# Second layer's modulation summed on VectorE beside the gate/up product, instead of by matmuls on TensorE

## What is computed

```python
c_act = jax.nn.silu(c)[:, None, :]
cc_act = jax.nn.silu(c_ctx)[None, None, :]
for i in range(DEPTH):                       # DEPTH = 2
    need_ctx_out = i < DEPTH - 1
    mx = jnp.split(c_act @ ada_w[i] + ada_b[i], 6, axis=-1)     # ada_w[i]: 1024 x 6144
    mc = jnp.split(cc_act @ ada_w[i] + ada_b[i], 6, axis=-1)
    h_x = modulate(rms_norm(x, norm1_g[i]), mx[0], mx[1])
    h_c = modulate(rms_norm(y_ctx, norm1_g[i]), mc[0], mc[1])
    ...
    x = x + mx[2] * out_x
    x = x + mx[5] * swiglu(modulate(rms_norm(x, norm2_g[i]), mx[3], mx[4]), ffn_w_in[i], ffn_w_out[i])
```

## Time and profile before

| | |
|---|---|
| median of 3 runs | 2474.78 us (2474.26 to 2474.81) |
| the profiled execution | 2470.74 us |
| its span in the profile | 2468.8 us |
| TensorE busy | 2395.5 us (97%), 14666 matmul records |
| VectorE busy | 1507.4 us (61%) |
| ScalarE busy | 1213.8 us (49%) |
| GpSimd busy | 145.5 us (6%) |
| moved by DMA | 398.29 MB, mean 161 GB/s |

### The profile page before, as it was taken

How to read it: one execution, slowest core, us unless ns; L and a number is a source line. 1 busy time by engine, 2 the same in 40 slices (tenths; PEclk the granted TensorE clock), 3 DMA queues, 4 the chain that set the end, 5 groups by cost and what they waited for, 6 DMA issues and landing times.

```text
span 2468.8 us, 40542 instructions
## 1 busy us (share of the span) xinstructions
PE 2395.5 (97%) x14666; PEld 2063.5 (84%) x14666; DVE 1507.4 (61%) x2244; ACT 1213.8 (49%) x1776; POOL 145.5 (6%) x121
## 2 busy tenths in 40 slices
PE   7998999999899988999999999999999999999999
PEld 6745788888788857888888999898888899989887
DVE  5376533322552466766776847777677666677875
ACT  4365422222343524654654577555555545865553
POOL 3000100000000000000000012010000000221000
PEclk9999999999999999999999999999999999999999
DMA  9485632333243414656665555356566565544654
GB/s 328 152 266 183 214 110 93 93 98 94 81 128 94 146 50 137 188 183 191 179 188 190 177 171 179 112 175 185 181 192 186 184 189 165 173 134 145 198 171 149
DMA packets 397629, 398.29 MB, mean 161 GB/s; under 512 B 17344, under 2 KB 394720, under 8 KB 397520
## 3 DMA queue, kind: packets, MB, share of 16 engines
q1 hardware_dynamic: 394656, 390.25, 51.4%
q0 software_dynamic: 2864, 6.58, 0.8%
HBM read 395.73 MB, written 1.05 MB: 161 GB/s over the span
## 4 chain that ended last, share of the span: by engine, by line
PE 90%; DVE 5%; ACT 2%; issue 2%; DMA 0%; POOL 0%; SPq 0%; DVEq 0%; ACTq 0%
PE acc L1014 27%; PE acc L1025 25%; PE acc L1018 23%; PE wk L1089 2%; PE acc L1089 2%; DVE w_lo L2170 2%; PE wk L1197 1%; PE acc L1525 1%; PE acc L1232 1%; PE wk L1232 1%; PE acc L1108 1%; PE wk L1215 1%; PE acc L1434 1%; PE wk L1434 1%; PE wk L1108 1%
## 5 line engine op out<-in xcount | busy, mean ns | idle before, releaser
L2170 DVE TENSOR_TENSOR w_lo<-raw,w_hi 128x1024 fp32r<-128x1024 f32 (+1 forms) x656 | 816.7, 1258 | 563.4 <-ACT w_hi L1573 561.8
L1573 ACT CAST w_hi<-raw 128x1024 fp32r<-128x1024 f32 (+1 forms) x650 | 664.1, 1034 | 481.5 <-PE acc L1025 373.4
L1025 PE MATMUL acc<-h_all,w_lo 128*128 128x256 f32 (+1 forms) x3696 | 575.0, 298 | 0.0
L1018 PE MATMUL acc<-h_all,w_hi 128*128 128x256 f32 (+1 forms) x3360 | 556.0, 318 | 11.1 <-DVE rot L2486 4.9
L1025 PEld LDWEIGHTS acc<-h_all,w_lo 128*128 128x128 f32 x3696 | 525.0, 191 | 40.5
L1018 PEld LDWEIGHTS acc<-h_all,w_hi 128*128 128x128 f32 x3360 | 487.9, 192 | 55.4 <-issue 13.5
L1014 PE MATMUL acc<-h_all,w_hi 128*128 128x512 f32 x2016 | 509.0, 395 | 4.5 <-DVE h_all L2294 4.5
L1014 PEld LDWEIGHTS acc<-h_all,w_hi 128*128 128x128 f32 x2016 | 365.0, 190 | 70.5 <-issue 4.7
L1014 PE MATMUL acc<-hid_all,w_hi 128*128 128x512 f32 x880 | 221.5, 392 | 0.0
L1014 PEld LDWEIGHTS acc<-hid_all,w_hi 128*128 128x128 f32 x880 | 156.8, 188 | 26.8
L1025 PEld LDWEIGHTS acc<-hid_all,w_lo 128*128 128x128 f32 x1056 | 152.6, 188 | 17.1
(11 more groups left out here) (390 smaller groups left out, 2180.7 us busy)
## 6 DMA issues: line engine op xcount, KB each, us to landing
raw<-in_w_in_dram SPq DMA_DIRECT2D x100, 512.0 KB, 4.0
raw<-in_ffn_w_in_dram SPq DMA_DIRECT2D x88, 512.0 KB, 3.6
raw<-in_ffn_w_gate_dram SPq DMA_DIRECT2D x88, 512.0 KB, 4.1
raw<-in_ffn_w_up_dram SPq DMA_DIRECT2D x88, 512.0 KB, 4.2
raw<-in_ffn_w_down_dram SPq DMA_DIRECT2D x80, 512.0 KB, 4.1
ring<-in_ada_w_dram SPq DMA_DIRECT2D x58, 512.0 KB, 5.9
raw<-in_ret_w_qkvg_dram SPq DMA_DIRECT2D x48, 512.0 KB, 3.6
raw<-in_ffn_w_out_dram SPq DMA_DIRECT2D x40, 512.0 KB, 3.4
```

Of the source, the lines that this page charges most:

```text
L1018: pe.matmul(outs[cb], w_hi[:, s, k, c], x[:, kk, t], start=(u == 0 and k == 0 and x is hi), stop=False, skip_group_check=True)
L1025: mm = pe.matmul(o, w_lo[:, s, k, cb * P:(cb + 1) * P], x[:, u * KCH + k, t], start=False, stop=(last and k == nk - 1), skip_group_check=True)
L1573: act.copy(w_hi[:, s, 0:nk, :], raw[:, s, 0:nk, :]).then_inc(hi_done, 1)
L2170: dve.tensor_tensor(w_lo[:, s, 0:nk, :], raw[:, s, 0:nk, :], w_hi[:, s, 0:nk, :], ALU.subtract).then_inc(lo_done, 1)
```

## The change

The second layer's 48 units leave TensorE's side stream. Their weights are loaded by GpSimd in 48 chunks of 128 rows by 1024 columns (512 KB each) into two new buffers `ada_l`; a load waits until the chunk two before has been used. VectorE multiplies each chunk by the column of c_act that belongs to its 128 rows and adds it up over the eight chunks of a vector: 8 sums (m = 0 and 1 for both conditions, m = 2 to 5 for x alone), 64 operations of 1024 columns, placed in gu0 after step and evacuation of units 4 to 11 and 16 to 23 (one chunk, two operations each) and 28 to 43 (two chunks, one operation each). The 128 partitions of each sum are added on TensorE by four matmuls, after gu0's units 11, 23 (two sums each), 31, 35, 39 and 43, 32 in all. They are turned after dn0's unit 3 and finished by VectorE after its unit 8. The sums lie in `rows`, so the three tables ahead, behind and since are loaded after the last sum. gu0 is unrolled on TensorE and VectorE. The 32 units that stay are spread over 2 steps each instead of 1.2: 2 in a call, the last at the 25th of 32 steps.

```diff
-FIRST = ["ada0a", "kv0", "q0", "ada0b", "ada1", "wo0", "ada1b", "gu0", "dn0", "rq", "rk", "rv", "rg", "rwo", "gu1", "dn1"]
+FIRST = ["ada0a", "kv0", "q0", "ada0b", "wo0", "gu0", "dn0", "rq", "rk", "rv", "rg", "rwo", "gu1", "dn1"]
...
-SIDE_START = 10
+SIDE_START = 16
...
-    return k * 12 // 10 - SIDE_START
+    return 2 * k - SIDE_START
...
+ADA1_CHUNKS = 6 * DC
+ADA1_SUMS = [(m, w) for m in range(6) for w in range(2 if m < 2 else 1)]
+def ada1_place(i):
+    g = (4 + i if i < DC else 8 + i) if i < 2 * DC else 28 + (i - 2 * DC) // 2
+    return g
+def ada1_ops(i):
+    return 2 * (i + 1) if i < 2 * DC else 2 * DC + i + 1
...
+ADA1_AFTER = {11: (0, 1), 23: (2, 3), 31: (4,), 35: (5,), 39: (6,), 43: (7,)}
...
             both_squares("wo0")
+            for i in range(ADA1_CHUNKS):
+                m, k = divmod(i, DC)
+                if i >= 2:
+                    pool.wait_ge(ada1_acc, ada1_ops(i - 2))
+                pool.dma_start(ada_l[:, i % 2, :], a["ada_w"][1][k * P:(k + 1) * P, m * D:(m + 1) * D]).then_inc(ada1_in[i % 2], 16)
+            pool.wait_ge(ada1_sum, len(ADA1_SUMS))
+            for n, name in enumerate(("ahead", "behind", "since")):
+                pool.dma_start(rows[:, n * 512:(n + 1) * 512], const(name)).then_inc(in_tabs, 16)
             both_squares("dn0")
...
-            product("wo0", tok=both, needs=lambda u, b: (o_done, PAIRS0), squared=True, sums_after=lambda: late_modulations(LATE, 70))
-            late_modulations(70, SIDE_UNITS)
-            product("gu0", tok=both, normed=(8 * 2, 8 * 3))
-            pe.wait_ge(ada_taken, STAGES + 3)
-            turn_modulations(std, 12, wk[:, 0, 0:48]).then_inc(ada_sum, 1)
+            product("wo0", tok=both, needs=lambda u, b: (o_done, PAIRS0), squared=True)
+            def next_modulations(g):
+                for n in ADA1_AFTER.get(g, ()):
+                    pe.wait_ge(ada1_acc, ada1_whole(n))
+                    for k in range(KCH):
+                        mm = pe.matmul(wk[32 * k:32 * k + 32, 0, 0:COLS], sum_pad[:, 31 - n:63 - n], ada1_s[ada1_tile(n)][:, k * COLS:(k + 1) * COLS],
+                                       start=(n == 0), stop=True, tile_position=(0, 32 * k), skip_group_check=True)
+                    mm.then_inc(ada1_sum, 1)
+            product("gu0", tok=both, normed=(8 * 2, 8 * 3), after=next_modulations)
...
+            def weighted(i):
+                m, k = divmod(i, DC)
+                dve.wait_ge(ada1_in[i % 2], 16 * (i // 2 + 1))
+                for w in range(2 if m < 2 else 1):
+                    n, q = ADA1_SUMS.index((m, w)), (ada1_ops(i - 1) if i else 0) + w
+                    total, landed, col = ada1_s[ada1_tile(n)], ada_l[:, i % 2, :], c_act[:, w * DC + k:w * DC + k + 1]
+                    if k == 0:
+                        if n >= 2:
+                            dve.wait_ge(ada1_sum, n - 1)
+                        dve.tensor_scalar(total, landed, col, None, ALU.mult).then_inc(ada1_acc, 1)
+                    else:
+                        dve.wait_ge(ada1_acc, q - (m < 2))
+                        dve.scalar_tensor_tensor(total, landed, col, total, ALU.mult, ALU.add).then_inc(ada1_acc, 1)
...
+            rest("gu0", gate_up("gu0", 2 * S, 0), None, [lambda: None] * J["gu0"].iters, beside=beside_gate_up)
             head("dn0", None, "gu0", gate_up("gu0", 2 * S, 0))
-            dve.wait_ge(ada_taken, STAGES + 4)
-            modulations(STAGES + 2, 1, mod[:, 1], 0, 48)
-            rest("dn0", residual("dn0", 0, 5))
+            rest("dn0", residual("dn0", 0, 5), None, [lambda: None] * J["dn0"].iters, beside=next_modulations)
```

More of the change, by code:

```diff
@@ L183 @@
 RING = 3 * SLOTS
-SPARE, TAIL, LATE = 53, 58, 60
+SPARE, TAIL = 29, 32
 def ringed_before(name):
@@ L254 @@
 X_START, X_MEM, X_MEM_NORM = 8, 12, 13
-SIDE = ("ada0b", "ada1")
+SIDE = "ada0b"
 def side_unit(k):
[L263 to L269, removed]
-SIDE_START = 10
+    return SIDE, k // JOBS[SIDE].body, k % JOBS[SIDE].body
+SIDE_UNITS = JOBS[SIDE].body * JOBS[SIDE].iters
+SIDE_START = 16
 STAGES = 4
@@ L375, in sem @@
             return st.enter_context(nc.semaphore(name))
+        ada_l = sb("ada_l", [P, 2, D])
         with ExitStack() as on:
@@ L491, in build @@
         load = [sem(f"load{k}") for k in range(SLOTS)]
-        ada_load = [sem(f"ada_load{k}") for k in range(5 * SLOTS)]
+        ada_load = [sem(f"ada_load{k}") for k in range(EXTRA + RING)]
         hi_done = sem("hi_done")
@@ L1051, in product @@
                     one(0, per)
-                    with pe.Fori(1, job.iters) as it:
+                    for it in range(1, job.iters):
                         one(it)
@@ L1400, in _, with turn_next @@
             attention("first", heads_first(), None, beside_first, SIDE_TURNS, opening)
-            product("wo0", tok=both, needs=lambda u, b: (o_done, PAIRS0), squared=True, sums_after=lambda: late_modulations(LATE, 70))
-            late_modulations(70, SIDE_UNITS)
-            product("gu0", tok=both, normed=(8 * 2, 8 * 3))
-            pe.wait_ge(ada_taken, STAGES + 3)
-            turn_modulations(std, 12, wk[:, 0, 0:48]).then_inc(ada_sum, 1)
-            product("dn0", hi=hid_hi, lo=hid_lo, tok=both, needs=lambda u, b: (hid_ok, min(2 * u + 2, 11)), squared=True)
+            product("wo0", tok=both, needs=lambda u, b: (o_done, PAIRS0), squared=True)
[6 more added lines that the diff above has]
+                    mm.then_inc(ada1_sum, 1)
+            def turn_next(g):
+                if g == 3:
+                    pe.wait_ge(ada_taken, STAGES + 2)
+                    for h in range(2):
+                        mm = pe.matmul(wk[:, 0, COLS + 32 * h:COLS + 32 * h + 32], std[:, h * P:(h + 1) * P],
+                                       ident[:, :].rearrange("p (k r) -> p r k", k=KCH)[:, 0:len(ADA1_SUMS), :], start=True, stop=True)
+                    mm.then_inc(ada_sum, 1)
+            product("gu0", tok=both, normed=(8 * 2, 8 * 3), after=next_modulations)
+            product("dn0", hi=hid_hi, lo=hid_lo, tok=both, needs=lambda u, b: (hid_ok, min(2 * u + 2, 11)), squared=True, after=turn_next)
             product("rq", normed=8 * 4)
@@ L1570, in split @@
                 act.wait_ge(load[s], job.loaded(l, it, p))
-                behind = J["ada1b"].body * J["ada1b"].iters if job is J["gu0"] and isinstance(it, int) and it == 0 else 0
-                act.wait_ge(units_used, job.unit(l, it, p) + 1 - behind)
+                act.wait_ge(units_used, job.unit(l, it, p) + 1)
                 act.copy(w_hi[:, s, 0:nk, :], raw[:, s, 0:nk, :]).then_inc(hi_done, 1)
@@ L2207, in head, with rest @@
                     prev_evac[1](prev_layer(prev, name, l), J[prev].iters - 1)
-            def rest(name, evac, l=None, between=(), first=LAG):
+            def rest(name, evac, l=None, between=(), first=LAG, beside=None):
                 job, late = J[name], evac[1] if isinstance(evac, tuple) else None
@@ L2215, in rest @@
                     evacuate(name, evac, l, 0, p - LAG)
+                    if beside:
+                        beside(p)
                 def one(it):
```

112 lines of the change are left out of this document (60 added, 52 removed).

## The result

The changed kernel takes 2483.57 us (median of 7 runs, 2479.66 to 2486.92), the kernel before, run beside it, 2474.26 us (2472.53 to 2476.09). The ratio is 1.0037, with a 95% interval of 1.0027 to 1.0046: slower by 9.3 us. The forecast was 2474.7 us with a range to 2482.5 us; the time lies above the range, and on the side of the rival "the loads are late". A second set of runs gave 2482.82 against 2473.75 us, 9.1 us.

The account below looks back on a forecast made before the run. TensorE was taken as the bound, busy 97% of the span. Terms -2.8 - 1.0 - 0.6 + 4.3 = -0.1 us, added to the 2474.78 us median, gave 2474.7 us; 8-in-10 range 2469.0 to 2482.5 us.

Parts of the forecast that it names:

- the loads are late: Rival, VectorE in gu0's units 28 to 43: landings from 4.55 us on stall TensorE, 2479 to 2488 us; chance 0.20.
- Attention and tail: Units removed beside the first attention's softmaxes give back 2.8 us, those after its last heads 1.0 us.
- the floor of the forecast: Attention, fourth score product to next value product: ScalarE sets about 4.6 us, maybe 4.5 us, however many units go.
- all removed work counts: Rival: ScalarE isn't the floor and the casts before gu0 move up, -5.75 us in all, 2469.0 us; chance 0.12.
- Hand-over: Between wo0 and gu0: ten removed units let the norm's reciprocal come 0.6 us earlier, at most 2.65 us.
- Matmuls: gu0 on TensorE: eight added groups of four small matmuls cost 4.3 us, bounds 3.4 to 4.6 us.
- The turn, the unrolled loop: dn0's turn replaces one of the same instruction count, and gu0's loop is unrolled on TensorE: nothing for either.
- The loads (0 in the forecast): gu0, units 28 to 41: with 3.9 us landings VectorE falls 6.8 us behind, hidden with 6.6 us left.
- The clock: Rival: idle TensorE before gu0 drops to half clock, slowing gu0's first block, 2477 to 2480 us; chance 0.10.

Follow-up runs that it names:

- the second execution: The changed kernel itself, unedited, run and profiled again in the third set beside the four-buffer kernel; 2482.82 us (6 runs).
- the one with twelve fillers: Changed kernel with four load buffers, plus twelve idle matmul units in the attention's emptied last quarter and tail; 2476.59 us, 1.0016 of the kernel before.
- the removal: Changed kernel without the 48 loads, 64 sums, 32 matmuls and their waits, so second-layer modulation isn't computed; 2470.54 us, 0.9986 of the kernel before.
- the spread one: Changed kernel with four load buffers and the first layer's units at 2.3 attention steps each in place of 2; 2479.14 us, 1.0022 of the kernel before.
- half loads: Changed kernel with its two buffers, all loads after the first two bringing only 256 KB; 2477.90 us.

## Why the prediction was wrong, step by step

**Attention and tail (-2.8, -1.0): right.** From the first units to the fourth score product of the last pair but one (at 208.43 us in both chains) the changed kernel needs 2.1 us less, from there to wo0 1.7 us less, both without the half-clock rows; together -3.8 us. From that score product to the next value product it is 213.03 - 208.43 = 4.60 us, the floor of the forecast (5.16 us before, with four units). The chain runs there through VectorE's maximum and then ScalarE's exponentials and copy, so the floor was as the earlier trace rows had it: the removed units that lay above it came back, the others didn't, and "all removed work counts" (-10 us with the hand-over) falls.

**Hand-over (-0.6): nearly right.** From wo0's first product to gu0's first whole one, less the half clock at its start (2.8 us), it is 71.80 - 2.83 = 68.97 us against 69.88 us: -0.9 us.

**Matmuls (+4.3): undersized.** 5.5 us. The groups cost what their rows said; the products behind them cost 0.23 to 0.26 us more each. The term lacked the follower.

**The turn, the unrolled loop (0): right.** gu0 with nothing added takes 228.50 us, dn0 with the turn 0.2 us more.

**The loads (0 in the forecast): the step that failed.** The rule by which they would hurt was right: a loop of sum, reaction and landing against TensorE's pace, deciding at a landing of 4.55 us, and 1.0 us of stall for each 0.1 us. By it, landings of 4.85 and 5.03 us give 3.0 and 4.8 us; 4.5 and 6.2 us were measured. The rule looked at one wait, unit 42's for its accumulator (2.3 and 2.6 us); the small matmuls' waits for their sums behind units 39 and 43 (1.7 and 3.2 us in all) it took as past. What failed was the choice of the landing: 3.9 us, of two loads alone at another time, over the row of 5.9 us. The landing that counted, 4.85 to 5.03 us, lay between, on the wrong side of the margin. The reaction was 0.28 us, at the top of what I had allowed. With the bound known to 0.1 us and the landing only to 2 us, a chance of 0.20 for this rival was too low. GpSimd being held up by VectorE isn't needed for it: on the chain GpSimd issues 0.28 to 0.46 us after the sum, mostly in the middle of VectorE's next operation. Once it is 1.09 us, at 509.68 us, just as a split of VectorE ends (508.50 to 509.72 us); the second execution has the same delay at the same place, and its cause is open.

**The clock: priced in the wrong place.** I looked for it before gu0. There it does fall (0.50 from 288 to 294 us) and costs nothing, hidden in the norm. It cost in the attention and at wo0's start, where units had filled TensorE between softmaxes, and in the opening: at 204 to 240 us all profiled kernels without these units showed at least one half-clock row on the chain, 1.3 to 4.4 us, the kernel before and the one with twelve fillers none. I had counted the units there as free to remove or as gain, never as cover. It isn't a peculiarity of the profiled executions: the granted clock of a whole run is 0.993 on the mean in the 92 runs of the kernel before, 0.991 in the ten of the removal, and 0.990 to 0.991 in every other kernel, the one with twelve fillers too. How much of it stands in the medians isn't settled: the removal gives 3.1 us by medians and 4.7 us without half-clock rows, so about 1.6 us. That the missing units cause it on the chain is argued from where it falls, and the fillers' runs don't prove it, since the place changes from one execution to the next.

The account by medians: -4.7 (removal) + 1.6 (clock) + 5.5 (matmuls) + about 6 (stall) = +8.4 us of the 9.1 to 9.3 us. The last 0.8 us isn't settled: behind dn0 the kernels without the half-clock row at 1184 us have 1811.6 to 1812.5 us against 1811.6. Most are within a few tenths of it; the highest, 0.9 us over it, is the second execution of the changed kernel. Nor does anything show why the clock falls in the opening (116 or 127 us): the one at 116 us comes ahead of any removed unit.

None of the versions that compute the modulation beats the kernel before. The removal that pays for all is worth 3.1 us by medians, and the 32 matmuls alone are 5.5 us. Fewer groups of them would need more tiles for sums; that wasn't tried.

## What to carry over

Where one work item waits for a buffer that the same item frees, write the loop down (use, reaction, landing) and compare it with the pace of its reader. If the margin is smaller than what is uncertain in the landing, a stall needs more than a rival's chance. Another spacing of the same loads gave back 4.8 of the 9.1 us here by the medians, at no cost in space.

Matmuls that lay beside TensorE's waits gave nothing when they were removed here, and they may also have held its clock up: before moving them, look at the granted clock and the busy time of the stretch that they leave. When a small operation of another shape is put into a stream, price the first product behind it too.

## What the runs showed of the hardware

Behind a group of four 32-column matmuls between 512-column products the next product took 0.23 us longer, behind eight of them 0.26 us (3.86 and 3.89 against 3.63 us).

Loads on GpSimd's queue beside a weight stream landed in 3.0 us (256 KB) and 4.6 us (512 KB) with up to two under way, and in 5.0 to 6.3 us (512 KB) with up to four; GpSimd issued one 0.28 us after the semaphore that it waited for.

After a wait of 2.5 us in the middle of a dense stream the granted clock went from 1.00 to 0.50 for some 3 us and cost 1.9 us in one execution; after waits of 2.3 and 2.6 us at the same place in two others it stayed at 1.00. Ahead of 220 us TensorE was busy for 1.6 us of 4 us in the changed kernel and for 2.2 us in the spread one, and the clock fell to 0.50; with 1.9 us (half loads) and 2.7 us (twelve fillers) it stayed at 1.00.
